# Moving the operands of TensorE's split-weight matmuls to address remainders of their own

## The reference

```python
x = x + cat(dilated_attention(q, k, v), rglru(conv(u)) * gelu(y)) @ w_out      # first block
x = x + cross_attention(norm(x) @ w_cq, mem @ w_ck, mem @ w_cv) @ w_co
x = x + relu(norm(x) @ w_mlp_in) ** 2 @ w_mlp_out                              # 1024 -> 4096 -> 1024
for l in range(2):                                                             # second block
    z = rmsnorm(x) @ w_in[l]                # mla, fnet, diff, hgrn2 inputs and 4 x 1024 gates
    merged = sum(sigmoid(gate_n) * (o_n @ w_branch[l, n]) for n in range(4))
    x = x + merged @ w_out[l]
    x = x + (silu(g) * u) @ w_down[l]       # 1024 -> 2 x 2816 -> 1024
```

## Time and profile before

| | before |
|---|---|
| median of the timed runs | 1295.81 us |
| the profiled execution, its own time | 1295.53 us |
| its span, first to last instruction | 1293.7 us |
| granted TensorE clock, mean | 0.994 |
| TensorE matmul busy | 1265.9 us, 9208 instructions |
| VectorE busy | 862.2 us |
| ScalarE busy | 652.5 us |
| moved by DMA | 211.77 MB, mean 164 GB/s |

### The profile page before, as it was taken

One profiled execution on the slowest core, in us unless ns is written; L12 is line 12 of the kernel. 1 busy time (PEld: TensorE's weight loads), 2 busy tenths in 40 slices (PEclk: granted clock), 3 DMA queues, 4 the chain that ended last, 5 costly groups with the idle time before them and its releaser, 6 DMA issues.

```text
span 1293.7 us, 22072 instructions
## 1 busy us (share of the span) xinstructions
PE 1265.9 (98%) x9208; PEld 1178.1 (91%) x9208; DVE 862.2 (67%) x1194; ACT 652.5 (50%) x1049; POOL 114.4 (9%) x152
## 2 busy tenths in 40 slices
PE   8999999999999999998999999999999999999998
PEld 8998999988788989997999998888899988999986
DVE  6897667644466675998656553667577996655543
ACT  5896655543368464342544443556552434544432
POOL 1100000000000000661000000000003810000000
PEclk8999999999999999999999999999999999999999
DMA  9543445555535323442555555433343325455552
GB/s 368 204 163 115 180 135 192 196 185 180 188 101 193 131 99 131 164 152 84 189 189 176 190 196 185 165 139 136 112 145 131 134 96 196 165 191 174 187 196 98
DMA packets 30324, 211.77 MB, mean 164 GB/s; under 512 B 3344, under 2 KB 3728, under 8 KB 5264
## 3 DMA queue, kind: packets, MB, share of 16 engines
q1 hardware_dynamic: 29936, 210.22, 45.5%
q10 hardware_dynamic: 288, 0.14, 0.0%
HBM read 209.29 MB, written 1.05 MB: 163 GB/s over the span
## 4 chain that ended last, share of the span: by engine, by line
PE 74%; DVE 13%; ACT 6%; issue 5%; DMA 1%; SPq 0%; DVEq 0%; ACTq 0%
PE bank L508 72%; DVE w_lo L1625 3%; ACT w_hi L1125 2%; DVE W L1599 2%; DMA ring<-weight_pieces 1%; ACT W L1125 1%; PE bank L608 1%; PE bank L843 1%; DVE xs L2125 1%; DVE W L1585 1%; DVE junk L2123 1%; DVE W L2105 1%; DVE W L1586 1%; DVE W L1617 0%; DVE stat L1558 0%
## 5 line engine op out<-in xcount | busy, mean ns | idle before, releaser
L1625 DVE TENSOR_TENSOR w_lo<-ring,w_hi 128x2048 fp32r<-128x2048 f32 x183 | 422.5, 2309 | 283.9 <-ACT w_hi L1125 283.5
L1125 ACT ACTIVATE w_hi<-ring 128x1024 fp32r<-128x1024 f32 (+1 forms) x368 | 366.2, 1046 | 241.9 <-PE bank L508 226.2
L508 PE MATMUL bank<-x_hi,w_hi 128*128 128x256 f32 x1840 | 267.2, 284 | 2.4 <-ACT w_hi L1125 2.4
L508 PE MATMUL bank<-x_hi,w_lo 128*128 128x256 f32 x1840 | 261.5, 281 | 1.0 <-DVE w_lo L1625 0.9
L508 PE MATMUL bank<-x_lo,w_hi 128*128 128x256 f32 x1840 | 254.8, 280 | 0.0
L508 PEld LDWEIGHTS bank<-x_hi,w_hi 128*128 128x128 f32 x1840 | 237.0, 189 | 5.7 <-issue 2.4
L508 PEld LDWEIGHTS bank<-x_hi,w_lo 128*128 128x128 f32 x1840 | 236.5, 188 | 2.3 <-DVE w_lo L1625 1.7
L508 PEld LDWEIGHTS bank<-x_lo,w_hi 128*128 128x128 f32 x1840 | 233.6, 188 | 0.0
L508 PE MATMUL bank<-W 128*128 128x128 f32 (+4 forms) x716 | 110.7, 327 | 8.3 <-ACT W L1125 4.8
L508 PEld LDWEIGHTS bank<-W 128*128 128x128 f32 (+3 forms) x716 | 87.8, 187 | 21.5 <-issue 12.3
L508 PE MATMUL bank<-w_lo,hid_hi 128*128 128x512 f32 x304 | 78.5, 394 | 0.0
(11 more groups left out here) (257 smaller groups left out, 1238.0 us busy)
## 6 DMA issues: line engine op xcount, KB each, us to landing
ring<-weight_pieces SPq DMA_DIRECT2D x191, 1024.0 KB, 4.8
const<-constants SPq DMA_DIRECT2D x1, 1376.5 KB, 8.9
W<-x_features SPq DMA_DIRECT2D x4, 256.0 KB, 5.2
ring<-weight_pieces SPq DMA_DIRECT2D x2, 512.0 KB, 6.0
h<-x SPq DMA_DIRECT2D x2, 512.0 KB, 11.9
W<-rg_weights SPq DMA_DIRECT2D x1, 1024.0 KB, 9.7
xs<-mem_features SPq DMA_DIRECT2D x1, 1024.0 KB, 11.4
oT<-mem SPq DMA_DIRECT2D x1, 1024.0 KB, 11.4
```

What stands on the lines that cost most here:

```text
L508: return nc.tensor.matmul(out, lhsT, rhs, start=first, stop=last)
L1125: return nc.scalar.activation(out, in_, ACT.Copy, scale=scale)
L1625: v.tensor_tensor(w_lo[:, q % SPLITS, 0:n], raw(pp)[:, 0:n], w_hi[:, q % SPLITS, 0:n].bitcast(F32), ALU.subtract).then_inc(s_weight_low, 1)
```

## The change and its diff

It touches addresses alone; no instruction is added, removed or reordered. `w_hi` and `w_lo` become four tensors of one slot each. The SBUF tensors are allocated in another order, with small unused tensors (`gap0` to `gap5`) between them.

```diff
-        ring = sb("ring", [P, RING, PIECE])
-        w_hi = sb("w_hi", [P, SPLITS, PIECE], F32R)
-        w_lo = sb("w_lo", [P, SPLITS, PIECE], F32R)
-        const = sb("const", [P, C_SIZE])
-        vec = sb("vec", [P, V_SIZE])
-        row = sb("row", [P, R_SIZE])
+        sb("gap0", [P, 10])
+        ring = sb("ring", [P, RING, PIECE])
+        x_hi = sb("x_hi", [P, KT, S], F32R)
         h = sb("h", [P, TT, D])
         xs = sb("xs", [P, TT, D])
-        x_hi = sb("x_hi", [P, KT, S], F32R)
-        x_lo = sb("x_lo", [P, KT, S], F32R)
         oT = sb("oT", [P, KT, S])
+        sb("gap1", [P, 2])
+        w_hi0 = sb("w_hi0", [P, PIECE], F32R)
+        sb("gap2", [P, 5])
+        x_lo = sb("x_lo", [P, KT, S], F32R)
+        sb("gap3", [P, 5])
+        w_hi1 = sb("w_hi1", [P, PIECE], F32R)
+        sb("gap4", [P, 12])
+        w_lo1 = sb("w_lo1", [P, PIECE], F32R)
+        sb("gap5", [P, 40])
+        w_lo0 = sb("w_lo0", [P, PIECE], F32R)
+        w_hi, w_lo = (w_hi0, w_hi1), (w_lo0, w_lo1)
         W = sb("W", [P, ARENA])
...
+        const = sb("const", [P, C_SIZE])
+        vec = sb("vec", [P, V_SIZE])
+        row = sb("row", [P, R_SIZE])
```

More of the change, by code:

```diff
@@ L166, in sem @@
             return ctx.enter_context(nc.semaphore(name))
+        sb("gap0", [P, 10])
         ring = sb("ring", [P, RING, PIECE])
-        w_hi = sb("w_hi", [P, SPLITS, PIECE], F32R)
-        w_lo = sb("w_lo", [P, SPLITS, PIECE], F32R)
-        const = sb("const", [P, C_SIZE])
-        vec = sb("vec", [P, V_SIZE])
-        row = sb("row", [P, R_SIZE])
+        x_hi = sb("x_hi", [P, KT, S], F32R)
         h = sb("h", [P, TT, D])
         xs = sb("xs", [P, TT, D])
-        x_hi = sb("x_hi", [P, KT, S], F32R)
+        oT = sb("oT", [P, KT, S])
+        sb("gap1", [P, 2])
+        w_hi0 = sb("w_hi0", [P, PIECE], F32R)
+        sb("gap2", [P, 5])
         x_lo = sb("x_lo", [P, KT, S], F32R)
-        oT = sb("oT", [P, KT, S])
+        sb("gap3", [P, 5])
[5 more added lines that the diff above has]
+        w_hi, w_lo = (w_hi0, w_hi1), (w_lo0, w_lo1)
         W = sb("W", [P, ARENA])
@@ L514, in first_gemm @@
                 bank = fill(job, "g")
-                hi, lo = (w[:, 0, :].rearrange("p (k c) -> p k c", k=KT) for w in (w_hi, w_lo))
+                hi, lo = (w[0][:, :].rearrange("p (k c) -> p k c", k=KT) for w in (w_hi, w_lo))
                 for half, kh in ((0, 0), (0, 1), (1, None)):
@@ L541, in gemm @@
                 bank = fill(job, group)
-                hi, lo = (w[:, q % SPLITS, 0:KT * n].rearrange("p (k c) -> p k c", k=KT) for w in (w_hi, w_lo))
+                hi, lo = (w[q % SPLITS][:, 0:KT * n].rearrange("p (k c) -> p k c", k=KT) for w in (w_hi, w_lo))
                 pe.wait_ge(s_weight_high, 2 * q + 1)
@@ L712, in _ @@
                         q = split_of[p]
-                        hi, lo = (w[:, q % SPLITS, :].rearrange("p (k c) -> p k c", k=4) for w in (w_hi, w_lo))
+                        hi, lo = (w[q % SPLITS][:, :].rearrange("p (k c) -> p k c", k=4) for w in (w_hi, w_lo))
                         pe.wait_ge(s_weight_high, 2 * (q + 1))
@@ L736, in _ @@
                             for k in range(KT):
-                                ins = mm(bank[:, 0:S], w[:, q % SPLITS, 32 * k:32 * k + P], x[:, k, :], i == k == 0, i == 2 and k == KT - 1)
+                                ins = mm(bank[:, 0:S], w[q % SPLITS][:, 32 * k:32 * k + P], x[:, k, :], i == k == 0, i == 2 and k == KT - 1)
                         full(ins, job)
@@ L752, in _ @@
                         q = split_of[p]
-                        hi, lo = (w[:, q % SPLITS, :].rearrange("p (k c) -> p k c", k=2) for w in (w_hi, w_lo))
+                        hi, lo = (w[q % SPLITS][:, :].rearrange("p (k c) -> p k c", k=2) for w in (w_hi, w_lo))
                         if j == 0:
@@ L1143, in split_ahead @@
                         cut = slice(half * n // 2, (half + 1) * n // 2)
-                        copy(w_hi[:, q % SPLITS, cut], raw(pp)[:, cut]).then_inc(s_weight_high, 1)
+                        copy(w_hi[q % SPLITS][:, cut], raw(pp)[:, cut]).then_inc(s_weight_high, 1)
             act.dma_start(vec[:], vec_d).then_inc(s_vec, 16)
@@ L1208, in _ @@
                                 act.wait_ge(s_first_loaded[half], 16)
-                                copy(w_hi[:, 0, cut], raw(0)[:, cut]).then_inc(s_weight_high, 1)
+                                copy(w_hi[0][:, cut], raw(0)[:, cut]).then_inc(s_weight_high, 1)
                                 continue
@@ L1624, in split_ahead @@
                     dve.wait_ge(s_weight_high, 2 * (q + 1))
-                    v.tensor_tensor(w_lo[:, q % SPLITS, 0:n], raw(pp)[:, 0:n], w_hi[:, q % SPLITS, 0:n].bitcast(F32), ALU.subtract).then_inc(s_weight_low, 1)
+                    v.tensor_tensor(w_lo[q % SPLITS][:, 0:n], raw(pp)[:, 0:n], w_hi[q % SPLITS][:, 0:n].bitcast(F32), ALU.subtract).then_inc(s_weight_low, 1)
             def product_low(m):
@@ L1708, in _ @@
                             dve.wait_ge(s_weight_high, half + 1)
-                            v.tensor_tensor(w_lo[:, 0, cut], raw(0)[:, cut], w_hi[:, 0, cut].bitcast(F32), ALU.subtract).then_inc(
+                            v.tensor_tensor(w_lo[0][:, cut], raw(0)[:, cut], w_hi[0][:, cut].bitcast(F32), ALU.subtract).then_inc(
                                 (s_first_low, s_weight_low)[half], 1)
```

## The result

The changed kernel takes 1297.32 us (median of 10 runs, 1295.78 to 1299.62), the kernel before 1295.18 us (10 runs beside them, 1293.39 to 1296.37). The ratio is 1.002, 95% interval 1.0011 to 1.0028. I had forecast 1274 us, with 75% on faster. The time is inside my range of 1240 to 1299 us, but it lies between the two cases that I had given little, "no change" (0.12) and "slower" (0.13).

The account below looks back on a forecast made before the run. The prediction took TensorE's matmul stream, 117.5 ns each in gate/up, to bound the kernel. Its terms, -17.5 - 1 - 3.2 = -21.7 us from 1295.8, gave 1274 us, range 1240 to 1299.

Parts of the forecast that it names:

- no change: Rival for the whole kernel: independent ports, or the same slow rhythm at the new distances; 1296 us, chance 0.12.
- slower: Rival for the whole kernel: reads only 32 bytes apart delay each other more often; mildest form 1303 us, chance 0.13.
- What bounds the kernel: Gate/up and down projections: TensorE has no idle time, its matmul stream sets the speed; clock at 1.00 throughout.
- That the distance sets the pace: TensorE matmuls: moving read and next weight load meet in memory; their distance decides which rhythm, 113.4 or 117.8 ns.
- the exchanged form: 1152 matmuls with moving and stationary operands swapped, some at 113.4 and some at 117.8 ns: -1 us, bounds 2.5 either way.
- My sign of being wrong: Gate/up: pace staying at 117 to 118 ns in both slots would mean the rhythm doesn't hang on the distance.
- I take 113.4 ns, the lower of the two rhythms seen, for five of six pairs: 5520 matmuls with x moving, w stationary: five pairs at 113.4 ns, one at 117.5; -17.5 us.
- The lowest pace: Matmuls of 256 columns: 108.8 ns, read from transposes of 128 columns, as the lowest defensible pace.
- all collisions gone: Rival: every pair of operands reaches 108.8 ns, about 1233 us; chance 0.13 for a gain of 35 to 65 us.
- How much gets through: x-moving, w-stationary matmuls: half the gain passes for 778 where VectorE is near its limit, all for the other 4742.
- Down: 912 down-projection matmuls of 512 columns: half of a 7 ns gain from 233.8 towards 226.8 ns, -3.2 us.
- The splits, ring, moved constants at 0: VectorE/ScalarE splits, weight-piece loads and moved constants: no cost, 0 us; splits bounded by 2 us either way.

Follow-up runs that it names:

- the small kernel: Not a changed kernel: only matmuls on copies of x, operand distance varied between groups; 256 float32r columns with 128 stationary took 113.3 to 120.1 ns in its first scan.
- the scan: Matmul-only kernel, 256 moving columns, operand distance varied: 120.0 ns at 0, 113.3 or 117.8 at 64 and 192, 117.4 to 120.1 at odd multiples of 32.
- The experiment with 160 bytes: Kernel before with x_hi and x_lo moved by 32 bytes and the arena padded, so x-moving, w-stationary distance is 160 instead of 192: 1306.54 us, ratio 1.0091.
- the sums at 64, 76 and 160 bytes: Kernel before, padded so the x-moving, w-stationary distance mod 256 is 64, 76 or 160 instead of 192: ratios 0.9925, 0.9865 and 1.0091.
- order alone: Changed kernel's tensor order and four separate slots, with gaps restoring every distance of the kernel before: 1294.62 us, ratio 0.9996 to the kernel before.

## Why the prediction was wrong, point by point

**What bounds the kernel: right.** TensorE stayed without idle time in gate/up and down, and each full kernel moved the way its matmul paces did. Only "throughout" was too much for the clock: the first 60 us had a granted clock of 0.94 (0.97 after).

**That the distance sets the pace: right.** It was read from `kr` and the exchanged form and holds in the small kernel with nothing else at work. My sign of being wrong, a pace that stays at 117 to 118 ns in both slots, would have misled: the mean stayed there, while the flat rhythm gave way to a pattern for each pair. My picture of why was only partly right. I had a 512-byte weight load meeting a 1024-byte moving read; with a quarter of the load the cost remained at 113.3 to 117.8 ns, though the pace at a given distance changed. What is shown is that the pace depends on where the two operands start and on the number of stationary columns, and that in bfloat16 the three distances tried do not differ. How the memory brings it about stays open.

**The step that failed: "I take 113.4 ns, the lower of the two rhythms seen, for five of six pairs".** I had written myself that no row showed an odd multiple of 32, and then filled the gap with the better of two paces seen at multiples of 64. Among the multiples of 32 in the scan, the faster rhythm came at 64 and 192 alone. In the changed kernel the five pairs at odd multiples of 32 ran at 117.6 to 119.1 ns and the sixth (320, that is 64 mod 256) at 117.4, near the slower of its two rhythms; whether its irregular neighbours keep it there was not tested. (For `x_lo,w_hi` slot 0 the prediction's list has 448 where the table of addresses gives 480. With 480 five of six are odd multiples of 32, as it says.) The term was -17.5 us, and it was +2.1. The experiment with 160 bytes changes this term by +11.9 us and the exchanged form by +3.0, and costs 0.9%.

**The lowest pace: wrong.** I took 108.8 ns from transposes because "they have the same weight load behind them". But the transposes are plain float32, whose pace before goes by the moving columns: 16 matmuls of 256 columns take (3.61 - 0.378) / 15 = 215 ns each, twice the transposes' pace at 128.

```profile
445.92 3.61 PE L508 MATMUL bank<-const,xs 128*128 128x256 f32 x16
...
L508 PE MATMUL bank<-const,xs 128*128 128x256 f32 x32 | 7.2, 378 | 0.0
```

So the row said nothing about 256 columns of `float32r`; no group of theirs with 128 stationary columns, at any of 64 distances, ran below 113.3. The forecast itself did not use 108.8, its lower bounds and the rival "all collisions gone" did.

**How much gets through: too much.** I let everything pass but half of 778 matmuls. Of the sums at 64, 76 and 160 bytes 69% to 75% arrived in the span, at granted clocks of 0.994 to 0.995 beside 0.994 before.

**The exchanged form: wrong sign.** -1 us forecast, +2.7 measured. It had been in the faster rhythm for about half of its matmuls, so a blind move had more to lose than I allowed; +2.5 was the bound I gave.

**Down: half right.** I said a faster rhythm at 226.8 ns was possible without having seen it; the pair at distance 0 ran at 226.6. One pair in six has it, so -1.2 us for -3.2 forecast. And 233.3 was not twice the slower rhythm: 512 columns have paces of their own (226.7 at distance 0, where 256 columns have 120.0), so the doubling that gave 226.8 was right by luck.

**The splits, ring, moved constants at 0: right.** VectorE's low half is at 2309 ns on both pages, the load at 4.8 us, and order alone changes nothing.

**The rivals.** "Slower" is the one that came in direction, 2.1 us for its 7, but not by its mechanism: the two pairs at 32 bytes gave 118.1 and 118.5, the one at 160 gave 119.1, so nearness is not the rule. Its sign, "from a mean pace of 117.7 ns on", was too low to tell anything, since the kernel before itself has a mean of 117.8.

**The rule of the skill.** The Trainium skill, "SBUF — State Buffer", "Who interferes with whom", has TensorE's two read ports independent. In bfloat16 the runs agree: 109.2 ns at three distances. In `float32r` they do not: 113.3 to about 122 ns by distance. "TensorE: Matmul & The Clock Gate", "Back-to-back issue gap", gives N / 2.4 + 2.5 ns for an isolated matmul of N columns, worked out 109.2 for 256 and 215.8 for 512. The stream of bfloat16 matmuls hits both; `float32r` exceeds them everywhere, at 256 columns by 4.1 ns at best.

## What to carry to other kernels

## What the runs showed of the hardware that was not expected

- A `float32r` matmul of 256 columns costs 113.3 to about 122 ns at the full clock, by the distance of its operands mod 256 bytes, where bfloat16 costs 109.2 at the three distances tried (0, 64, 192); 512 columns cost 226.7 to 240 for bfloat16's 215.8.
- Some distances (64, 192) have two stable rhythms, 113.3 and 117.8 ns. One held for nearly a thousand matmuls; which one it is can differ between stages of one execution. Distance 76 too was seen at 113.3 and at 120.0.
- Moving both operands together by a multiple of 32 bytes changes nothing, by 4 to 28 bytes it does: at distance 76, 113.4 became 116.7 to 121.4 ns.
